# Attention units squared one unit ahead, more modulation chunks among them, and expert sharing sums laid out by channel quarter

## The reference, cut to what matters

```python
def adaln(cvec, w, b):
    m = jax.nn.silu(cvec) @ w + b                       # w: 1024 x 6144 for each layer
    return [t[:, None, :] for t in jnp.split(m, 6, axis=-1)]

def attn_in_proj(h, w_in, q_norm, kv_norm, w_q_up, w_kv_up, q_gain, k_gain, na_q_gain, na_k_gain):
    p = h @ w_in
    ...
    q = rmsnorm((rmsnorm(q_lat, q_norm) @ w_q_up).reshape(B, L, MLA_HEADS, QK_DIM), q_gain)
    ckv = rmsnorm(kv_lat, kv_norm)
    k, v = mla_expand(ckv, k_rope, w_kv_up, k_gain)     # a norm per head again
    nq = rmsnorm(na_qkv[:, :, 0], na_q_gain)
    nk = rmsnorm(na_qkv[:, :, 1], na_k_gain)

def hier_moe(h, w_grp, b_grp, w_rt, b_rt, w_gate, w_up, w_down):
    ...                                                 # gates: two experts of one group per token
    hg = jnp.einsum('nd,edf->nef', t, w_gate)
    hu = jnp.einsum('nd,edf->nef', t, w_up)
    return jnp.einsum('nef,efd->nd', jax.nn.silu(hg) * hu * gates[:, :, None], w_down)
```

## Time and profile before

| what | value |
|---|---|
| time, median of 3 runs (lowest, highest) | 1317.21 us (1314.58, 1325.98) |
| the profiled execution: its time, its span | 1313.93 us, 1312.2 us |
| PE busy, granted clock (share of full) | 1158.4 us (88%), 0.924 |
| DVE, ACT, POOL busy | 582.9, 265.3, 210.9 us |
| moved by DMA | 317.34 MB, mean 242 GB/s |
| chain that ended last, by engine | PE 81%, DMA 6%, DVE 5%, issue 2%, SPq 2% |
| attention units from the first q unit, pairs | 139.48 to 192.25 us, 192.25 to 309.71 us |
| expert loops | 415 to 655 us and 1041 to 1297 us |

### The profile page before, as it was taken

The page is one execution under the profiler, slowest core; times in us unless marked ns, Lnnn a source line. Parts: engine busy times, 40 slices in busy tenths (PEclk is TensorE's granted clock), DMA queues, the critical chain, the costliest instruction groups (busy, mean ns, idle before and its releaser), DMA issues.

```text
span 1312.2 us, 26081 instructions
## 1 busy us (share of the span) xinstructions
PE 1158.4 (88%) x9139; PEld 678.4 (52%) x9140; DVE 582.9 (44%) x1209; ACT 265.3 (20%) x644; POOL 210.9 (16%) x257
## 2 busy tenths in 40 slices
PE   3799867989955899999979999999986699999996
PEld 3554445755454455555555654344545455555553
DVE  0123342453342444444454334677644344444445
ACT  1111232432101111211132212222011111212111
POOL 1024220000111222222200001111010122222221
PEclk9699977999958999999989999899995799999998
DMA  9624139996284999999942313000038499986893
GB/s 316 227 78 175 65 139 351 328 372 230 79 363 183 418 392 395 417 410 377 396 172 66 126 37 125 0 0 1 0 106 373 186 404 421 413 372 254 322 423 160
DMA packets 83502, 317.34 MB, mean 242 GB/s; under 512 B 11160, under 2 KB 12097, under 8 KB 58089
## 3 DMA queue, kind: packets, MB, share of 16 engines
q1 hardware_dynamic: 78730, 304.95, 59.7%
q0 software_dynamic: 1952, 6.90, 1.3%
q10 hardware_dynamic: 2752, 4.53, 0.9%
HBM read 307.82 MB, written 8.54 MB: 241 GB/s over the span
## 4 chain that ended last, share of the span: by engine, by line
PE 81%; DMA 6%; DVE 5%; issue 2%; SPq 2%; POOL 1%; ACT 1%; POOLq 0%; DVEq 0%
PE banks L431 78%; DMA arena<-in_ada_b 3%; DVE arena L952 3%; DMA arena<-slot_rows 2%; SPq L1827 1%; PE banks L598 1%; POOL slot_rows L1731 1%; DMA mod_rows<-arena 1%; DMA slot_rows<-arena 1%; SPq L1825 1%; PE banks L482 1%; PE banks L793 0%; DVE arena L998 0%; POOL arena L1720 0%; PE banks L546 0%
## 5 line engine op out<-in xcount | busy, mean ns | idle before, releaser
L431 PE MATMUL banks<-arena 128*32 128x128 f32 (+9 forms) x8712 | 1101.5, 420 | 90.0 <-DMA arena<-in_ada_b 17.4
L431 PEld LDWEIGHTS banks<-arena 128*32 128x32 f32 (+4 forms) x8712 | 623.1, 155 | 541.4 <-issue 386.7
L952 DVE TENSOR_TENSOR arena<-banks,arena 128x64 f32<-128x64 f32 (+4 forms) x284 | 114.0, 413 | 111.6 <-PE banks L431 77.1
L952 DVE TENSOR_TENSOR arena<-arena 128x384 f32<-128x384 f32 (+11 forms) x229 | 153.8, 677 | 4.4
L1207 DVE SCALAR_TENSOR_TENSOR arena<-arena 128x768 f32<-128x768 f32 x81 | 83.2, 1027 | 92.1 <-issue 87.9
L1748 POOL COPY arena<-arena 128x256 f32 x79 | 66.2, 838 | 186.3 <-PE banks L431 147.0
L1581 ACT ACTIVATE arena<-banks 128x512 f32<-128x512 f32 x79 | 47.2, 597 | 241.2 <-PE banks L431 241.2
L1739 POOL TENSOR_TENSOR arena<-arena 128x256 f32<-128x256 f32 x81 | 59.4, 733 | 219.2 <-PE banks L431 219.2
L1217 DVE TENSOR_SCALAR arena<-arena 128x64 f32<-128x64 f32 x79 | 15.4, 195 | 167.5 <-ACT arena L1585 167.5
L1719 POOL TENSOR_SCALAR arena<-arena 128x8 f32<-128x8 f32 (+2 forms) x28 | 10.4, 372 | 384.2 <-ACT arena L1440 266.5
L1306 DVE TENSOR_SCALAR arena<-arena 128x385 f32<-128x385 f32 x24 | 11.6, 482 | 82.4 <-ACT arena L1642 82.4
(11 more groups left out here) (144 smaller groups left out, 460.0 us busy)
## 6 DMA issues: line engine op xcount, KB each, us to landing
arena<-in_moe_w_gate SPq DMA_DIRECT2D x64, 1024.0 KB, 8.2
arena<-in_moe_w_up SPq DMA_DIRECT2D x64, 1024.0 KB, 10.5
arena<-in_moe_w_down SPq DMA_DIRECT2D x64, 1024.0 KB, 10.5
arena<-in_ada_w SPq DMA_DIRECT2D x24, 2048.0 KB
arena<-in_hy_w_in SPq DMA_DIRECT2D x6, 2048.0 KB
arena<-in_attn_w_in SPq DMA_DIRECT2D x3, 2048.0 KB
arena<-slot_rows SPq DMA_DIRECT2D x6, 1024.0 KB, 7.3
arena<-mod_rows SPq DMA_DIRECT2D x8, 512.0 KB, 9.6
```

Of the source, the lines that this page charges most:

```text
L431: return pe.matmul(out, lhsT, rhs, start=start, stop=stop, skip_group_check=True)
L952: return dve.tensor_tensor(o, p, q, op)
```

## The change

The change has three parts.

1. In the units TensorE and ScalarE work two units ahead instead of one, with PSUM banks given out by hand, and VectorE reduces the squares of unit n+1 (`mean_squares`) before it multiplies unit n, so that GpSimd's power of n+1 runs beside the multiplication of n.
2. Seven chunks instead of two follow units 6 to 12 and 13 instead of 18 lie among the pairs. The ring's order is a function `place_of`: items 9 to 14 use slots 0 and 1 by turns while `up` holds slot 2. The bias table of the neighbourhood attention is loaded earlier, and GpSimd's masks on it lie between the powers of units 1 and 2 and of 3 and 4.
3. In the expert loop a bank now holds one channel quarter of token tiles 0 and 1 (four banks) or two quarters of tile 2 (two banks). The first half is eight share matmuls and the second half four; only the last two of them go to a bank that another row quarter wrote in the first half.

```diff
+        def place_of(n):
+            return n % 3 if n < 9 else (n - 9) % 2 if n < 15 else (n + 2) % 3
...
+        def share_sum(l, t, q, n=1):
+            b = place["acc", l * 6 + (q if t < 2 else 4 + q // 2)]
+            c = (t if t < 2 else q % 2) * DE
+            return ps[:, b, c:c + DE] if n == 1 else ps[:, b:b + 2, c:c + DE] if t < 2 else ps[:, b, :].rearrange("p (q c) -> p q c", q=2)
...
-        at_unit = {7: chunks[0], 9: chunks[1]}
-        at_pair = {int(1.32 * n) + 1: c for n, c in enumerate(chunks[2:])}
+        at_unit = {6 + n: c for n, c in enumerate(chunks[:7])}
+        at_pair = {int(1.9 * n) + 1: c for n, c in enumerate(chunks[7:])}
...
-                produce("nq", 0)
+                produce(*units[0])
+                produce(*units[1])
                 for n, (kind, t) in enumerate(units):
-                    if n + 1 < len(units):
-                        if units[n + 1] == ("q", 0):
+                    if n + 2 < len(units):
+                        if units[n + 2] == ("q", 0):
                             for tt in range(T):
                                 produce("nv", tt)
...
-                        produce(*units[n + 1])
+                        produce(*units[n + 2])
                     if n in at_unit:
-                        ada(*at_unit[n])
+                        ada(*at_unit[n], 7)
                     turn_unit(kind, t)
...
-                first = turn[0]
-                acc = []
-                for i in range(6):
-                    t, hf = i // 2, i % 2
-                    acc.append((("acc", l * 6 + i), [("xffn", l * 3 + t)], (first + 2 + i) % 8))
+                first = turn[0] + turn[0] % 2
+                acc = [(("acc", l * 6 + i), [("xffn", l * 3 + (1 if i < 4 else 2))], (first + 2 + i) % 8) for i in range(6)]
...
-                def share_half(half, shares, rows_, start):
-                    for t in range(T):
-                        for hf in range(2):
-                            q = 2 * hf + (t + half) % 2
-                            o = ps[:, place["acc", l * 6 + t * 2 + hf], (q % 2) * DE:(q % 2 + 1) * DE]
-                            last = mm(o, shares[32 * q:32 * q + 32, t * P:(t + 1) * P], rows_[32 * q:32 * q + 32, :], start, False)
+                def share_parts(parts_, shares, rows_, start):
+                    for t, q in parts_:
+                        o = share_sum(l, t, q)
+                        last = mm(o, shares[32 * q:32 * q + 32, t * P:(t + 1) * P], rows_[32 * q:32 * q + 32, :], start, False)
                     return last
                 def first_half(shares, rows_, start=False):
-                    share_half(0, shares, rows_, start).then_inc(s_["moe_half"], 1)
+                    two = ((2, 0), (2, 2), (0, 1), (0, 3), (0, 0), (0, 2), (1, 1), (1, 3))
+                    share_parts(two, shares, rows_, start).then_inc(s_["moe_half"], 1)
                 def second_half(g, shares, rows_, start=False):
                     pe.wait_ge(s_["moe_half"], g + 1)
-                    return share_half(1, shares, rows_, start).then_inc(s_["moe_shared"], 1)
+                    return share_parts(((1, 0), (1, 2), (2, 1), (2, 3)), shares, rows_, start).then_inc(s_["moe_shared"], 1)
...
+                mean_squares(0)
+                for n, (kind, t) in enumerate(units):
+                    if n + 1 < len(units):
+                        mean_squares(n + 1)
+                    if n - 1 in at_unit:
+                        ada_row(at_unit[n - 1])
+                    b = n % 2
                     sig("hrs").at(dve, n)
...
-                if n >= 3:
-                    wait_used(sp, items[n - 3])
-                s = item_loaded[n % 3]
+                held = [m for m in range(n) if place_of(m) == place_of(n)]
+                if held:
+                    wait_used(sp, items[held[-1]])
+                s = item_loaded[place_of(n)]
```

87 lines of the change are left out of this document (46 added, 41 removed).

## The result

The changed kernel takes 1302.24 us (median of 4 runs, 1298.49 to 1303.42) against 1321.60 us of the kernel before in its 4 runs: ratio 0.990, 95% interval 0.985 to 0.994. The forecast was 1265 us with a range of 1250 to 1286. The direction was right; two thirds of the gain are missing.

The account below looks back on a forecast made before the run. The prediction took TensorE, busy 97%, to bound the expert loops with weight loads barely in time, and a VectorE chain to hold the attention units. Sum: 1313.93 - 17 - 35.7 + 4 = 1265.2, forecast 1265 us, range 1250 to 1286.

Parts of the forecast that it names:

- Front, -17: Attention units and the pairs after them: both stages together were forecast to change by -17 us.
- Units: Attention units: five more chunks, a late load and a lower clock were to make them +2.4 us.
- the wait at unit 10: Attention units: the gate's load stands ahead of unit 10's chunk, so TensorE waits 4 us there.
- just in time: Attention units: with two slots, a chunk's 5 us load starts one unit, 5.5 us, before it is wanted.
- Pairs: Pairs after the units: a removed wait, its slow clock and five fewer chunks were to give -19.5 us.
- Edits at nothing: Bias table's load, GpSimd's four masks and the ring's new places were claimed to cost and gain nothing.
- Expert loop, -35.7: Expert loops: fewer share-matmul passes save 0.43 us a step over 79 steps, plus 1.7 us behind the loops.
- the sentence on the queue of instructions: Between experts: register work starts when the second half fits the queue; four matmuls fewer bring it forward as much.
- the first rival: Between experts: register work starts where it did, each of 64 experts' first steps saves nothing; 27.5 us back; chance 0.12.
- the picture is the one that the prediction had named as its sign: Expert loop: steps of 5.5 us within one expert beside 5.9 from expert to expert would show a wrong term.
- Loads, +4: Expert weight loads: 4 us of waiting, nearly all in the first loop's last four experts; bounds 0 to 10.
- loads set the first loop: First expert loop: 88 MB of weights take 227 us, so its end stays; 16 us back, 1281; chance 0.06.

Follow-up runs that it names:

- e1: Kernel before with only part 3, the new share-sum layout in the expert loop; 1314.1 us, ratio 1.000 to the kernel before.
- e12: Kernel before with part 2 alone: chunks moved and new ring order, units still one ahead, bias table not loaded earlier; 1301.4 us, ratio 0.988.
- e11: Kernel before with part 1 alone: units two ahead, plus the earlier bias table and masks, chunks and ring as before; 1300.3 us, ratio 0.984.
- e18: e16 run again, on the same chip as e17; 1260.7 us, ratio 0.958 to the kernel before.
- e16: e15 with the front of e11, so two chunks among the units and eighteen among the pairs; 1260.7 us, ratio 0.961 to the kernel before.
- e17: e16 with share sums laid out as before, halves of six and six, signal behind the sixth; 1272.2 us, ratio 0.966 to the kernel before.
- e4: Changed kernel with the second half's signal given by the first half's second share matmul instead of its eighth; 1280.8 us, ratio 0.975 to the kernel before.
- e7: Changed kernel run again with nothing altered; 1299.1 us, ratio 0.986 to the kernel before.
- e13: Changed kernel with TensorE's repeating expert-loop code placed at slot 0 of a code-fetch block; 1301.1 us, ratio 0.992 to the kernel before.
- e14: Changed kernel with TensorE's repeating expert-loop code placed at slot 128, about half a block further than e13; 1302.0 us, ratio 0.991 to the kernel before.
- e9: Changed kernel with e4's early signal and next-expert register loads split around the down product; 1274.4 us, ratio 0.967 to the kernel before.
- e10: e9 with the gate's load moved behind the ring's last item; 1266.9 us, ratio 0.960 to the kernel before.
- e15: e10 with register numbers also loaded ahead and carried across groups of four experts; 1267.5 us, ratio 0.967 to the kernel before.
- e3: Changed kernel with two TensorE waits ahead of the transposing sums exchanged, ScalarE's down product first; 1289.1 us, ratio 0.983 to the kernel before.

## Why the prediction was wrong, by its own steps

**Front, -17: right in sum, partly by luck.** -18.3 at the end of the pairs. The two terms that I had priced gave -14.6, and the rest came from one taken at nothing. Units were taken at +2.4 and measured +5.9: the wait at unit 10 is 5.32 us (4 taken), and two more of 0.69 and 2.09 stand before it; "just in time" for the two slots was late by these. Pairs were taken at -19.5 and measured -20.5. Projections ahead of the units, taken at nothing, ended 3.7 us sooner. Kernels with the bias table's load at its old place show 1.3 and 0.8 (e1, e12), those with the earlier load 2.5 to 6.0: some 3 us of gain that I had put at zero. But the split was misread: e11 shows that the units two ahead, with the bias table's earlier load, give the whole gain, and that the chunks' move, which I had priced as the gain of the pairs, adds nothing beside them. What five chunks cost the units, 18.7 us, is close to what I had counted (12.5 of work, 4 of waiting, 2.4 of clock); I had not asked what the units and pairs take if they stay.

**Edits at nothing: one wasn't.** Behind the first loop VectorE now has to read three tiles instead of two before it has freed TensorE's next banks. From its first read to TensorE's next matmul: 638.61 to 647.00 us, 8.4 us; before, 659.19 to 664.84, 5.7 us. TensorE's timeline, after and before:

```profile
647.00 3.33 PE L444 MATMUL banks<-arena 128*128 128x128 f32 x14 [8.46 <-DVE arena L966]
```

```profile
664.84 7.65 PE L431 MATMUL banks<-arena 128*128 128x128 f32 x48 [5.70 <-DVE arena L991]
```

A few instructions later the difference has grown to 3.0 us. From the last step's start to that first read the changed kernel is 2.1 us shorter, which pays most of it back. I had not looked at who waits for the banks. The other 3.2 us between the loops are a lower clock in the Hyena part, the same place before and after:

```profile
908.00:918.00 10.00, 9.12 (x26) 3.59 (x25) 8.74 (x13) 1.33 (x3) 2.30 (x2) 1.00 0.00 0
```

```profile
893.00:903.00 10.00, 9.12 (x18) 3.37 (x17) 6.88 (x12) 1.19 (x2) 0.00 (x0) 0.73 0.00 0
```

The change isn't its cause: ten of the twenty traces show the fall and ten don't, and of two traces of one kernel e18's does and e16's doesn't. What brings it is open.

**Expert loop, -35.7: the step that failed.** The 0.43 us of the array are right (0.406, e17 against e18), and so is the reading of the 12 share matmuls. What failed is the sentence on the queue of instructions: "I read its start as the moment when the second half fits into the queue, and four matmuls fewer should bring it forward as much" (two matmuls fewer, which are four records). e4 shows that the sequencer stood at the wait for the first half. That wait has the same end in both kernels; four fewer records in the second half bring the register work 0.09 us forward, and the 1.87 us behind it lie bare. The row for it stood in view: the earlier trace rows have 0.3 us between the full-array loads and the registers, and that is as well the end of the first half plus the issue of six matmuls. Steady steps gave 0.16 x 79 = 12.6 us instead of 34. This is the first rival, given 0.12 with up to 27.5 us back, and the picture is the one that the prediction had named as its sign: steps of 5.5 us within an expert beside 5.9 from expert to expert.

**First passes: a term that the sum had not.** Slow steps at the loops' starts were in sight before, and I took them as fixed. Above 13 steady steps they cost 6.7 and 5.3 us before, 13.1 and 16.2 after, 9.3 and 15.1 in its repetition: 12 to 17 us of the gain. Shown is that they stand in the pass in which code is fetched, that a second trace of one program repeats most of them (e7), and that the placement of the code moved one loop by 8 us (e13, e14). Why they grew is open. That the shortened step let them grow was only argued: e11, with the old steps, has 13.8 us in its second loop. That early register work shrinks them fits e9, e10 and e15, and not the second loops of e16 and e18.

**Loads, +4: right in place, late in force.** In the changed kernel nothing waits for them. Once steps take 5.50 us, they hold the first loop at 217 to 218 us whatever TensorE does (e9's first 13 steps take 79.4 us and e15's 75.6, and both loops 217.5): of the 15.0 us (37 x 0.406) that part 3 would give that loop, 13 to 14 are lost (e17 against e16 and e18). So the rival "loads set the first loop", given 0.06 and 16 us back, describes the kernel that I thought I was predicting; had the sequencer not stood, the forecast would still have been some 10 us too low (an estimate: 14 lost against the 4 taken). 7.45 us for 3.15 MB are 422 GB/s, where the earlier trace rows have 418.

**The rest**: the mean granted clock is 0.924 before and 0.922 after; in the loops no step was changed by it apart from those behind a stand. With the loops' 79 steady gains of 0.16 us and 12 to 17 us lost at their starts, the loops come out level, as measured.

## What to carry to other kernels

Before a matmul is taken out of a loop, find what TensorE's sequencer does between the last wait and the next step's first instruction, and measure that serial piece from the wait and not from the end of the work before it: the array can only gain the cover that this piece doesn't need. A semaphore should be signalled by the last instruction that its waiter depends on, and numbers for a branch be loaded where the sequencer is ahead of the array; both together took 28 us off the changed kernel (e9), part of it at the loops' starts. Where work is moved into a stage with room, try first whether making the room isn't the whole gain.

## What the runs showed of the hardware that I had not expected

- A wait carried by a matmul holds back what stands behind it in TensorE's instruction stream, register work too: its start moved by 0.15 us with the signal (e4), and not at all with an earlier explicit wait (e3).
- Matmuls are issued at 0.045 to 0.049 us each (eight in 0.39 us in e4; the register work is 0.09 us later with two more).
- A loop's first pass cost 1 to 21 us more than its steady rate for 13 steps (e17's first loop, e14's second); one stand was 7.62 us (e13). Behind the first pass no code was fetched (the changed kernel's second loop, 1110 to 1200 us).
- One core's loads ran at 415 to 421 GB/s to the first loop's end (windows of e9, e17 and e18, DMA share 1.01 to 1.02), and 7.44 to 7.48 us an expert was the same in every kernel that reached it (e9, e10, e15, e16 and e18).
